# Attention output with V held in the array and head pairs interleaved, in a one-core encoder block

## The reference, cut to what matters

```python
q = (rmsnorm(c_q, q_norm) @ w_uq).reshape(B, S, MLA_HEADS, MLA_NOPE + MLA_ROPE)
k_nope = (ckv @ w_uk).reshape(B, S, MLA_HEADS, MLA_NOPE)
v = (ckv @ w_uv).reshape(B, S, MLA_HEADS, MLA_V)             # 8 heads x 64
def block(args):                                             # Q_BLOCK = 128 queries
    s = (jnp.einsum('bqhd,bkhd->bhqk', qn, k_nope) + jnp.einsum('bqhd,bkd->bhqk', qr, k_rope))
    pr = jax.nn.softmax(s.astype(jnp.float32) * scale, axis=-1).astype(v.dtype)
    return jnp.einsum('bhqk,bkhd->bqhd', pr, v)
...
a = mla_branch(...) @ w_branch_mla[i]
bm = mlstm_branch(...) @ w_branch_ml[i]
g_a, g_b = jnp.split(jax.nn.sigmoid(gates), 2, axis=-1)      # gates = a slice of u @ w_in
mixed = (g_a * a + g_b * bm) @ w_out[i]
```

## Time and profile before

| | us |
|---|---|
| median of three runs | 1301.32 |
| the three runs | 1300.29 to 1301.88 |
| the profiled execution's own time | 1301.57 |
| its span, first to last instruction | 1299.7 |
| PE busy | 1254.9 |
| DVE busy | 675.6 |
| ACT busy | 424.3 |

### The profile page before, as it was taken

The page is one execution under the profiler, slowest core; times in us unless marked ns, Lnnn a source line. Parts: engine busy times, 40 slices in busy tenths (PEclk is TensorE's granted clock), DMA queues, the critical chain, the costliest instruction groups (busy, mean ns, idle before and its releaser), DMA issues.

```text
span 1299.7 us, 15628 instructions
## 1 busy us (share of the span) xinstructions
PE 1254.9 (97%) x5910; PEld 1033.9 (80%) x5910; DVE 675.6 (52%) x1043; ACT 424.3 (33%) x612; POOL 118.5 (9%) x96
## 2 busy tenths in 40 slices
PE   7999999999989999999999999899999999999996
PEld 6888888888867867777788878778888888888785
DVE  6644444442257866646446486485444443222774
ACT  5323232311134343435411433243232322112552
POOL 3000000000024000001101200230000000000343
PEclk9999999999989999999999999899999999999997
DMA  5433333232222321110311123214232323333101
GB/s 190 130 98 96 97 97 97 97 97 97 97 59 49 100 79 34 33 37 30 114 49 49 33 89 107 65 50 128 83 110 82 112 81 112 97 97 111 52 17 65
DMA packets 96866, 107.75 MB, mean 83 GB/s; under 512 B 15062, under 2 KB 87478, under 8 KB 96822
## 3 DMA queue, kind: packets, MB, share of 16 engines
q1 hardware_dynamic: 96608, 107.10, 26.5%
q10 hardware_dynamic: 214, 0.05, 0.0%
HBM read 105.04 MB, written 2.10 MB: 82 GB/s over the span
## 4 chain that ended last, share of the span: by engine, by line
PE 84%; DVE 7%; issue 4%; ACT 2%; POOL 2%; DMA 0%; SPq 0%; DVEq 0%; POOLq 0%; ACTq 0%
PE bank L283 24%; PE bank L285 23%; PE bank L284 23%; PE bank L879 2%; PE bank L893 2%; DVE v_lo L456 1%; PE bank L411 1%; PE bank L512 1%; DVE tbuf L449 1%; PE bank L507 1%; PE bank L901 1%; PE bank L377 1%; PE bank L508 1%; PE bank L290 1%; POOL sqacc L397 1%
## 5 line engine op out<-in xcount | busy, mean ns | idle before, releaser
L313 DVE TENSOR_TENSOR w_lo<-w_raw,w_hi 128x1024 fp32r<-128x1024 f32 x195 | 241.9, 1246 | 374.0 <-ACT w_hi L306 366.8
L283 PE MATMUL bank<-v_hi,w_hi 128*128 128x512 f32 x968 | 381.3, 394 | 0.3 <-ACT og L1396 0.3
L285 PE MATMUL bank<-v_hi,w_lo 128*128 128x512 f32 x968 | 377.4, 390 | 0.0
L284 PE MATMUL bank<-v_lo,w_hi 128*128 128x512 f32 x968 | 377.2, 390 | 0.0
L306 ACT ACTIVATE w_hi<-w_raw 128x1024 fp32r<-128x1024 f32 x195 | 203.8, 1054 | 364.3 <-PE bank L285 360.7
L285 PEld LDWEIGHTS bank<-v_hi,w_lo 128*128 128x128 f32 x968 | 182.0, 188 | 38.4
L283 PEld LDWEIGHTS bank<-v_hi,w_hi 128*128 128x128 f32 x968 | 182.2, 188 | 38.0 <-ACT og L1396 0.5
L284 PEld LDWEIGHTS bank<-v_lo,w_hi 128*128 128x128 f32 x968 | 182.2, 188 | 37.6 <-issue 0.2
L285 PE MATMUL bank<-prod_hi,w_lo 128*128 (+1 forms) x352 | 136.9, 389 | 0.0
L283 PE MATMUL bank<-prod_hi,w_hi 128*128 (+1 forms) x352 | 136.9, 389 | 0.0
L284 PE MATMUL bank<-prod_lo,w_hi 128*128 (+1 forms) x352 | 136.9, 389 | 0.0
(11 more groups left out here) (271 smaller groups left out, 1405.8 us busy)
## 6 DMA issues: line engine op xcount, KB each, us to landing
w_raw<-in_ffn_w_gate SPq DMA_DIRECT2D x44, 512.0 KB, 3.6
w_raw<-in_ffn_w_up SPq DMA_DIRECT2D x44, 512.0 KB, 3.5
w_raw<-in_ffn_w_down SPq DMA_DIRECT2D x44, 512.0 KB, 3.4
w_raw<-in_w_in SPq DMA_DIRECT2D x32, 512.0 KB, 3.7
w_raw<-in_w_out SPq DMA_DIRECT2D x8, 512.0 KB, 3.2
w_raw<-in_ple_w_gate SPq DMA_DIRECT2D x8, 512.0 KB, 3.3
x_tm<-in_x SPq DMA_DIRECT2D x4, 512.0 KB, 7.3
w_raw<-in_w_branch_mla SPq DMA_DIRECT2D x4, 512.0 KB, 3.3
```

The costliest lines, as they stand in the source:

```text
L283: nc.tensor.matmul(o, whi, a_hi, start=start, stop=False)
L284: nc.tensor.matmul(o, whi, a_lo, start=False, stop=False)
L285: return nc.tensor.matmul(o, wlo, a_hi, start=False, stop=stop)
L313: nc.vector.tensor_tensor(w_lo[:, s, :], w_raw[:, s, :], w_hi[:, s, :].bitcast(F32), ALU.subtract).then_inc(w_lo_done, 1)
```

## The change

The probabilities are normalised before they are transposed, and the output is made directly with features on the partitions, for two heads at a time.

- Order: the 32 blocks are now numbered s with `head_block(s)`; even steps belong to the pair's first head, odd steps to its second, so eight steps make a pair of heads. The loop has 36 steps, and the transposes of block t run at step t + 4.
- DVE takes one reciprocal for each block, ACT multiplies the block's `Pm` by it in place (`norm`), and the transposes wait for that.
- The copies of the transposed blocks go to two tiles that hold a whole pair: ACT's to `scratch` (first head), DVE's to `PT_odd` (second head).
- `pair_output`: for each pair, eight matmuls with 64 columns of `Vm` held in the array and 512 query columns of the transposed probabilities moving. The first head's four accumulate in partitions 0 to 63 of bank 7, the second's in 64 to 127, in turns. `O`, `o_out`, `pv` and the 16 transposes of `O` are gone, and `oT_hi` and `oT_lo` are made from bank 7 once per pair.
- Each gate chunk is cut into four quarters of six products (`fm_quarter`), one per step from step 4 on. `pair_output` stands at steps 12, 20 and 28, between the point where a gate pair is complete and its banks' next use, and once more after the loop.
- The convolution's 20 taps stand singly at the ends of DVE's steps 6 to 25.
- The banks of MV and MO change, and `mb(0)` now waits for the first of the four `og` evictions.

The core of the diff:

```diff
-    O = ar("O", [P, TB, S], 64.5)
-    PT = ar("PT", [P, 2, S], 72.5)
+    PT_odd = ar("PT_odd", [P, TB, S], 64.5)
...
+    def fm_quarter(n, half, banks, kk):
+        for f in range(2):
+            k, c = 4 * half + kk, kk * 256 + f * P
+            last = three(B[banks[f]][:], wv(n, c, c + P), v_hi[:, k, :], v_lo[:, k, :], k == 0, k == KD - 1)
+        return last
...
+        def p_transposes(t):
+            pe.wait_ge(ms["norm"], t + 1)
+            if t >= 2:
+                pe.wait_ge(ms["pt_even"] if t % 2 == 0 else ms["pt_odd"], t // 2)
             for kb in range(TB):
-                last = nc.tensor.matmul(B[7][:, b * VDIM:(b + 1) * VDIM], PT[:, t % 2, kb * P:(kb + 1) * P],
-                                        Vm[:, kb, hh * VDIM:(hh + 1) * VDIM], start=(kb == 0), stop=(kb == TB - 1))
+                last = nc.tensor.transpose(B[5 + t % 2][:, kb * P:(kb + 1) * P],
+                                           Pm[:, t % 4, kb * P:(kb + 1) * P], ident[:])
+            last.then_inc(ms["pT"], 1)
+
+        def pair_output(pr):
+            pe.wait_ge(ms["pt_even"], 4 * pr + 4)
+            pe.wait_ge(ms["pt_odd"], 4 * pr + 4)
+            if pr >= 1:
+                pe.wait_ge(ms["oT_split"], pr)
+            for kb in range(TB):
+                for e in range(2):
+                    hd = 2 * pr + e
+                    last = nc.tensor.matmul(B[7][64 * e:64 * e + 64, :], Vm[:, kb, hd * VDIM:(hd + 1) * VDIM],
+                                            (scratch if e == 0 else PT_odd)[:, kb, :], start=(kb == 0),
+                                            stop=(kb == TB - 1))
             last.then_inc(ms["pv"], 1)
...
+        for s in range(STEPS + 4):
+            if s < STEPS:
+                scores(s)
+            if s >= 4:
+                p_transposes(s - 4)
+                if s >= 12 and s % 8 == 4:
+                    pair_output(s // 8 - 1)
+                c, kk = (s - 4) // 4, s % 4
+                if kk == 0:
+                    pe.wait_ge(w_lo_done, GAC + c + 1)
+                    if c % 2 == 0 and c >= 2:
+                        pe.wait_ge(ms["ga"], c)
+                last = fm_quarter(GAC + c, c % 2, [0, 1], kk)
+                if kk == 3:
+                    last.then_inc(w_used, 1)
+        pair_output(3)
+
+        MVB, MOB = [5, 2, 3, 4], [7, 0, 1, 6]
...
         pe.wait_ge(ms["q_split"], 6)
+        pe.wait_ge(ms["mo"], 1)
         mb(0)
...
+    def head_block(s):
+        return 2 * (s // 8) + s % 2, s % 8 // 2
```

DVE's step s, after the maximum and `nb` of block s:

```diff
+            if s in (12, 20, 28):
+                ga_out(s // 8 - 1)
+            if 2 <= s < STEPS + 2:
+                r = s - 2
+                dve.wait_ge(ms["exp"], r + 1)
+                if r >= 4:
+                    dve.wait_ge(ms["norm"], r - 3)
+                nc.vector.reciprocal(rsum[:, r % 4:r % 4 + 1], sums[:, r:r + 1]).then_inc(ms["rsum"], 1)
+            if s >= 14 and s % 8 == 6:
+                oT_low(s // 8 - 1)
+            if s >= 4 and s % 2 == 1:
+                t = s - 4
+                dve.wait_ge(ms["pT"], t + 1)
+                nc.vector.tensor_copy(PT_odd[:, :, head_block(t)[1] * P:(head_block(t)[1] + 1) * P],
+                                      v4(B[6][:])).then_inc(ms["pt_odd"], 1)
+            if s % 4 == 1 and s >= 5:
+                lo_upto(dve, GAC + (s - 5) // 4 + 3)
+            if s >= 6 and s - 6 < 4 * CONV:
+                conv_tap(dve, s - 6)
```

ACT's step s, after the exponential of block s:

```diff
+            if t >= 0 and t % 2 == 0:
+                bt = head_block(t)[1]
+                if t >= 8 and t % 8 == 0:
+                    act.wait_ge(ms["pv"], t // 8)
+                nc.scalar.activation(scratch[:, :, bt * P:(bt + 1) * P], v4(B[5][:]), ACT.Copy).then_inc(ms["pt_even"], 1)
+            if 2 <= s < STEPS + 2:
+                q = (s - 2) % 4
+                act.wait_ge(ms["rsum"], s - 1)
+                act.wait_ge(ms["exp"], s - 1)
+                nc.scalar.activation(Pm[:, q, :], Pm[:, q, :], ACT.Copy, scale=rsum[:, q:q + 1]).then_inc(ms["norm"], 1)
+            if s >= 14 and s % 8 == 6:
+                oT_high(s // 8 - 1)
+            if s % 4 == 0 and s >= 4:
+                hi_upto(act, GAC + (s - 4) // 4 + 3)
```

168 lines of the change are left out of this document (55 added, 113 removed).

## The result

| | before | after |
|---|---|---|
| median, four runs each, us | 1301.6 | 1281.32 |
| the runs | 1300.29 to 1302.43 | 1279.8 to 1281.55 |
| the profiled execution's own time | 1301.57 | 1281.55 |
| its span | 1299.7 | 1279.7 |
| first scores to first MV product | 123.27 | 103.40 |

The ratio is 0.9843 (0.9826 to 0.986): faster by 20.3 us, where 17.0 were forecast. The time lies 3.0 us under the forecast of 1284.3 and 0.2 us under the low end of the range. Nearly all of the gain lies in the attention stretch, 19.87 us of it; another 0.2 lies ahead of it, where the first scores start at 473.33 instead of 473.52, and what stands behind it has hardly moved in sum (0.1 more).

What follows compares the result with a forecast made beforehand. PE was taken as the bound. The attention stretch built from zero gave 105.5 us against 123.3, -17.8, and + 0.7 made -17.1; 1301.57 - 17.1 - 0.25 gave about 1284.3 us, range 1281.5 to 1298.5.

Steps and rivals of the forecast that it cites:

- The bound: Whole kernel: PE's own program plus its waits sets the time; waits of DVE and ACT are room for added work.
- Price of the pair's matmuls: Pair output in the attention loop: the two heads overlap on the array's halves, 3.7 us a pair, 14.8 in all.
- rival (a): Pair output: the halves do not overlap, the pairs cost 27.5 us instead of 14.8, total 1297.0; chance 0.22.
- Rival (b): Pair output: no overlap, and each turn between halves costs 0.11 us, 7.0 on 64 instructions, total 1304.0; chance 0.11.
- Rival (c): Attention loop: halves overlap but PE waits 0.3 us in each of 32 steps, 9.6 instead of 1.8, total 1292.1; chance 0.10.
- The gate eviction: Before step 12's quarter: 1.4 us plus the maximum, ending under transposes and pair output, 4.1 us.
- The step: One PE step of the attention loop: scores 0.86, transposes 0.44, six gate products with switch 6 x 0.227 + 0.09, 2.75 us.
- Its switch: From transposes to gate products: the first product takes 0.08 us more; 32 switches instead of 8, 2.0 us added.
- The first of the prediction's two sums: PE's losses and gains added up from the old kernel: -16.0 us.
- The new multiplication: ACT's normalising pass for each block: priced at 0.54 to 0.78 us.
- Behind the loop: After attention: 0.5 us lost at `mb(0)`'s wait for the first `og` copy, 0.2 at MO's first chunk; together 0.7.
- MO's wait: MO's first chunk waits 0.84 us for a weight split; the wait stays, with a loss of 0.2 us.

Runs made afterwards that it cites:

- same_half: The changed kernel with both heads of a pair accumulated in partitions 0 to 63 of bank 7, in one group: 1295.37 us, ratio 0.9947 to the kernel before.
- output_twice: The changed kernel with every pair's eight output matmuls issued twice in a row: 1295.52 us, ratio 0.9948 to the kernel before.
- taps_together: The changed kernel with the five taps of each convolution tile in one piece, at steps 9, 13, 17 and 21: 1289.62 us, ratio 0.9897 to before.
- whole_chunks: The changed kernel with each gate chunk whole again, 24 products at every fourth step instead of quarters: 1291.37 us, ratio 0.9911 to before.
- output_later: The changed kernel with the pair's output behind the first quarter of the next gate chunk instead of ahead of it: 1291.17 us, ratio 0.9909 to before.
- heads_apart: The changed kernel with one head's four output matmuls first, then the other's, instead of in turns: 1288.5 us, ratio 0.9894 to the kernel before.

## Why the prediction came out as it did

The mechanisms held; the size was too small. The two profiled executions differ by 20.0 us, where 17.1 were forecast. Of the 2.9 us between, 2.1 lie in the stretch, 0.6 behind it and 0.2 ahead of it. Point by point:

- **The bound.** Right: PE before and after, with DVE's and ACT's waits as room. ACT took 18.9 us more in the stretch, and PE's recorded waits for it are 0.7 us.
- **Price of the pair's matmuls.** Forecast 3.7 each, measured 3.58 and some 0.1 ahead of it. `same_half` shows that without overlap it would have been 7.0 (forecast for that case 6.9), and the kernel 1295.4, where rival (a) had 1297.0: that sum had the same term too much as the forecast's. The Trainium skill, TensorE: Matmul & The Clock Gate, section on packing small matmuls, gave with its 2.38 for three tiles an estimate of 17.4 us for four pairs; the four took 14.3, 14.7 with the entry. Two column tiles of 64 reached 7.01 / 3.58 = 1.96 of an ideal 2, where that section's three reached 79%.
- **Rival (b), a price for each turn.** None: `output_twice` added 3.43 a pair for sixteen instructions. TensorEngine Tiling of the Trainium skill, Key Properties, has a drain for a change of mode and none for a change of tile; the trace agrees, with 0.24 us a pair (0.15 + 0.09) for both changes of mode together.
- **Rival (c), late feeding.** It did not occur in after: PE's waits before the transposes are 0.7 us as recorded. By all that the distances between starts show they are about 1.5 in the loop and 0.4 at its start, where 1.8 + 0.4 were forecast. It was near: `taps_together` and `whole_chunks` make it appear with 8 to 9 us, each by moving work and adding none. The prediction's view of slack in sums (21.9 of 25.7 us) could not have told that; the step-by-step carrying forward of DVE's work did.
- **The gate eviction** ending under transposes and pair output: right, and `output_later` gives what this place is worth, 6.3 us of waits and a fall of the clock.
- **The step: the term that failed.** 2.75 was forecast and 2.67 to 2.69 measured. Its switch, 0.08 behind transposes, was taken from a row where the first product is longer and added to a transposes' distance of 0.44 from a row where `pv` follows. Behind transposes with a product to follow, the distance is 0.36. Summed over the stretch, the distances behind transposes are 2.2 us below the forecast. The quarters are 0.9 above it (1.475 each instead of 1.45), the pairs 0.5 below, the waits in the loop 0.3 below and the scores 0.1 below: 2.2 in all, which is 105.6 (the forecast's terms add up to 105.56) less 103.4. So the transposes' term alone is as large as the miss of the stretch, and the other four nearly cancel. The first of the prediction's two sums, which it did not take, has two such slips: 28 scores behind `pv` at 0.06 where before has 20 (1.2 us, not 1.7), and 2.0 for 24 switches that `whole_chunks` shows to cost 0.8. Before's own trace had a place that shows it, ahead of an MV chunk:

```profile
631.55 1.04 PE L950 MATMUL bank<-ident,mqk 128*128 128x128 f32 x8
632.34 0.48 PE L290 MATMUL bank<-w_hi,v_hi 128*128 128x512 f32 x1
632.66 0.40 PE L291 MATMUL bank<-w_lo,v_hi 128*128 128x512 f32 x1
```

  Eight transposes take 0.79 before a product, 0.87 before other transposes (630.68 to 631.55 in the same view), and the product 0.32: what the transposes give and what the product takes are both in these rows.
- **The new multiplication.** Priced at 0.54 to 0.78, measured 0.715, near the upper end. Nothing hung on it.
- **Behind the loop.** Forecast +0.7. The wait at `mb(0)` is 0.87 (0.8 was forecast) and costs about 0.3, not 0.5. MO's wait is 0.72 instead of 0.84, so a loss of 0.2 was forecast where 0.1 was gained. Together that is 0.2 up to `mb(1)` and 0.1 in the sums to the end, some 0.6 less than forecast. That the sums come this close is partly luck, since each holds one fall of the clock at another place.
- **The range.** The low end was drawn 2.8 us below the forecast, from feeding waits between 0 and 5 and nothing for an error in the step. A term that is repeated 28 to 32 times deserved its own margin: 0.08 each is 2.2 to 2.6 us, nearly the whole distance to that end. The time lies 0.2 us outside, less than one kernel differs from itself between two comparisons, but the forecast itself was 3.0 us off.

What stays open: why the clock falls at one wait in one run and at another in the next, what sets how far ahead PE starts the other half's matmuls, and the last 0.1 us of entering the 64-column form, which no run took apart.

## What to carry to other kernels

Where a matmul leaves half of the array's columns unused, hold the narrow operand, put two independent ones in turns on the two halves, and read the gain from the distance to the next instruction. A long piece of PE work is worth most between an eviction and the next use of its banks, and reordering that looks good by itself can lose until such a piece exists, so parts of such a change should be judged together and taken apart afterwards. When unit costs are taken as distances between starts, take each pair of neighbours from one place in the trace: a distance includes part of what follows.

## What the runs showed of the hardware

- Two matmuls of the same PE queue on different column halves start 0.01 us apart, each at its full rate of 0.43 us for 512 columns of `f32` as two instructions a product; at half clock 0.85, still side by side.
- PE started matmuls of one half ahead of three earlier ones of the other half, and no further (`heads_apart`: the second head starts beside the first head's fifth of eight instructions, 5.35 us a pair between 3.58 and 7.01).
- A matmul of 64 held columns costs what one of 128 costs, 0.43 an instruction; only its weight load is shorter, 0.137 against 0.188.
- Going from four `f32` transposes to the gate's products costs 0.03 us net: the transposes' distance is 0.08 shorter and the six products are 0.11 longer (after against `whole_chunks`).
- After the same wait of 0.87 us the granted clock went to half in two of ten profiles; in five it did 165 to 180 us behind the first MV product, in three at neither place.
